# A three-part model in one kernel: zeros on TensorE ahead of the weights, block products from the third channel tile on, the router's product by halves, identity products among the last rows

## The chip, the cores and the metric

The kernel runs on one core of a Trainium2 chip. The metric is the device time of one execution in microseconds. All data is float32. Each float32 matrix product appears in the trace as two records.

## The reference, cut to what matters

For 256 tokens of 1024 values the model runs two layers and then a third block:

```
for l in range(2):
    proj = x @ w_in                        # 8 groups of columns
    q, k, v = silu(causal_dwconv(...))     # 4 taps
    o_a = gated_delta_rule(...)            # chunks of 64 tokens, 4 heads
    o_b = causal attention, 8 heads, partial rotary
    x = layer_norm(alpha * x + concat(o_a, o_b) @ w_out)
    hid = causal_dwconv(x @ w_up) + b      # 3 taps, 2 x 2816 columns
    x = layer_norm(alpha * x + (silu(gate) * val) @ w_down)
h = rms_norm(x); differential and dilated attention on h @ w_in_2
x = x + concat(oa, od) @ w_out_2
h = rms_norm(x); aff = softmax(h @ w_router)        # 16 experts
for e in range(16):                        # the 32 best tokens of each
    x[idx[e]] += ((silu(h[idx] @ w_gate[e]) * (h[idx] @ w_up[e])) @ w_down[e]) * gate
out = rms_norm(x)
```

## The kernel before, in words

All engines' instruction streams are written out by hand, in one function per engine, and joined by semaphores. SyncE (SP) streams the weights: through a ring of four slots (`slot_in0` to `slot_in3`) in the layers, and through four larger slots (`piece_in0` to `piece_in3`) for the experts. A slot is loaded again when a count of products says that it is free.

**Start.** SP loads the first column block, half of the transposed input, and the second block (semaphore `second_columns`, L401), and later, in its order, the columns of the convolution weights (L412). ScalarE's queue issues the other half of the input (L1470) and the identity constants (L1471). GpSimd's queue issues a table of distances and two small bias rows (L519 to L521), and waits for slot 1 before the other constants (L523). TensorE's `first_products` (L816) waits for the first block and goes on through L826, L813, L831, L676 to L901, L861, L909 (it needs the copied logits, L1516) and L916 (it needs ScalarE's second SiLU, L1494). ScalarE's first tap (L1482) needs the convolution columns.

**Up-products of a layer.** The 2 x 2816 hidden channels are made in 22 tiles of 2 x 128 channels. The first `AHEAD` = 3 tiles are direct: `up(j, t)` (L1098, instructions of L676) takes 16 products of 128x128 for one half t of the tokens, so 32 for the tile, into the banks `UP_BANKS`. From the fourth on a tile is made by seven block products (`up_block_products`, L1101, instructions of L1123) of four 128x128 products each, so 28. They need sums of weight blocks, which GpSimd makes tile by tile (`up_sums`, L526; four instructions, L536 to L541, with drains between), and sums of token blocks, which VectorE makes once (L2082 to L2087). VectorE joins the seven results (`up_summed`, L2094) into a bank, from where ScalarE (L1615) and VectorE (L2126) convolve. GpSimd begins once the output product is done; in layer 1 it first issues eleven DMAs (L586 to L598).

The x rows of the second half of the tokens come later from the layer norm than those of the first. So TensorE first makes `up(0, 0)` and `up(1, 0)`, then waits for `x_rows`, transposes the second half (`second_tile`, L661), makes `up(2, 0)`, and waits for the transposed copies (L666). Then follow the three second halves, and the block tiles with j = 3 on.

**Router.** The output product of the third block (L1261) makes two halves of tokens of two halves of columns each, k by k with both column halves inside. VectorE adds both column halves to x (`second_rows`, L2200), TensorE transposes x (`rows_transposed`, L1231), one copy goes to ScalarE (L1648) and one to VectorE (L2211), and TensorE makes the logits (L1244). `keep_clock` (L1248) issues products with the identity, whose results nobody reads: one behind the logits, four behind the affinities' transposes (L1270). VectorE selects the tokens (L2242, L2244), and the rows are gathered.

**Experts.** Expert 0 begins with L1348. SP loads a slot again when `piece_used` has counted its last product. The last half of the last expert's rows comes in four loads (L508, `LAST_ROWS`), with a semaphore each; TensorE's `down_rows` (L1312, instructions of L1316) takes them as they land.

Of the kernel before, what the change touches and what calls it, by code (L numbers as in the profile page):

```python
# [12 lines left out]
P = 128  # L13
S = 256
T = S // P
# [56 lines left out]
UP_BANKS = (0, 1, 4)  # L72
PAIR_BANKS = {0: (4, 5), 1: (0, 1)}
FIRST_PAIR_BANKS = (6, 7)
# [7 lines left out]
AHEAD = 3  # L82
ROWS_BANKS = (2, 3, 6, 7)
H2_BANKS = (0, 1, 4, 5)

HID_BANKS, OUT_BANK = (3, 4, 6), (4, 0)
# [82 lines left out]
def build(nc, a, out, scratch, CAT):  # L169
    ctx = ExitStack()  # L170
    with ctx:
# [125 lines left out]
        normed_rows = second_scratch.take(T, D)  # L297
        out_quarters = second_scratch.take(D // 4)
# [219 lines left out]
        def _(pool):  # L518
            pool.dma_start(bucket_table[0:BUCKETS + 1, :], a["bias_table"]).then_inc(sem("bias_in"), 16)  # L519
# [124 lines left out]
        def _(pe):  # L644
# [196 lines left out]
            for l in range(DEPTH):  # L841
# [259 lines left out]
                def up_block_products(j):  # L1101
# [57 lines left out]
            for n in range(AHEAD):  # L1159
                if n % 2 == 0:  # L1160
                    unit_in(L, n // 2)
                if n == AHEAD - 1:
# [4 lines left out]
            for n in range(AHEAD):  # L1167
# [63 lines left out]
            def rows_transposed(t):  # L1231

                pe.wait_ge(sem("second_rows"), t + 1)
                for kh in range(2):
# [4 lines left out]
            def logits(t, ks):  # L1239

                if ks[0] == 0:
                    pe.wait_ge(sem("h2_copied"), 2 * t + 2)
                for k in ks:
                    last = mm(ps[2 + t][:, 0:NE], xT[:, k, t * P:(t + 1) * P], router_w[:, k, :], start=(k == 0), stop=(k == KT - 1))  # L1244
# [9 lines left out]
            for t in range(T):  # L1254
                for k in range(4):
                    if t == 0:
                        pe.wait_ge(sem("attended_read"), at(L, "attended_read", k + 1))
                    elif k == 1:
                        rows_transposed(0)
                    for nh in range(2):  # L1260
                        last = mm(ps[ROWS_BANKS[2 * t + nh]][:, :], mixT[:, 4 + k, t * P:(t + 1) * P], slot(7, 1024)[:, k, nh * 512:(nh + 1) * 512], start=(k == 0), stop=(k == 3))  # L1261
                last.then_inc(sem("rows_used" if t else "rows_t0"), 2 if t else 1)
            logits(0, range(6))
            rows_transposed(1)
            logits(0, range(6, KT))
            logits(1, range(KT))
            keep_clock(1)
# [40 lines left out]
            def keep_clock_on_rows():  # L1308

                mm(ps[1][:, :], ident, normed_rows[:, 0, 0:512], start=True, stop=True)  # L1310
# [16 lines left out]
            def expert(n_, ahead):  # L1327
# [102 lines left out]
        def _(act):  # L1430
# [39 lines left out]
            act.dma_start(xT[:, 0:4, :], a["x_t"][:, 0:4, :]).then_inc(sem("xT_in0"), 16)  # L1470
            act.dma_start(const[:, 0:2 * P + 4], a["consts"][:, 0:2 * P + 4]).then_inc(sem("ident_in"), 16)  # L1471
            for l in range(DEPTH):
# [131 lines left out]
                for j in range(FT):  # L1604
# [4 lines left out]
                    else:  # L1609
                        act.wait_ge(sem("up_summed"), at(l, "up_summed", j - AHEAD + 1))  # L1610
                        act.wait_ge(sem("hidden_ready"), at(l, "hidden_ready", j - 2))
# [22 lines left out]
            def rms(n, t):  # L1634
# [3 lines left out]
                elif n == 1:  # L1638
                    act.wait_ge(sem("second_rows"), t + 1)
# [6 lines left out]
                if n == 1:  # L1646
                    act.wait_ge(sem("h2_transposed"), 2 * t + 1)
# [68 lines left out]
        def _(v):  # L1716
# [148 lines left out]

            for l in range(DEPTH):
# [227 lines left out]
                def up_summed(j):  # L2094

                    pair = FIRST_PAIR_BANKS if j == AHEAD else PAIR_BANKS[j % 2]
# [103 lines left out]
            def second_rows(t):  # L2200
# [3 lines left out]
                else:  # L2204
                    v.wait_ge(sem("rows_used"), (DEPTH + 1) * ROW_UNITS + 2)
                for nh in range(2):
                    xs = x[:, t, nh * 512:(nh + 1) * 512]
                    last = w.tensor_add(xs, xs, ps[ROWS_BANKS[2 * t + nh]][:, :])
                last.then_inc(sem("second_rows"), 1)
                v.wait_ge(sem("h2_transposed"), 2 * t + 2)  # L2210
                w.tensor_copy(xT[:, 4:8, t * P:(t + 1) * P], ps[H2_BANKS[2 * t + 1]][:, :].rearrange("p (x y) -> p x y", y=P)).then_inc(sem("h2_copied"), 1)  # L2211
# [137 lines left out]
```

## Time and profile before

| | |
|---|---|
| median of 3 runs | 2190.2 us (2189.45 to 2190.91) |
| profiled execution, own time | 2190.44 us |
| its span | 2188.7 us |
| TensorE busy | 1678.1 us, 77% |
| VectorE busy | 644.2 us, 29% |
| ScalarE busy | 310.7 us, 14% |
| GpSimd busy | 255.5 us, 12% |
| moved by DMA | 695.12 MB, mean 318 GB/s |

Times in the views are microseconds from the start of the span. "PE" is TensorE's products, "PEld" its weight loads, "DVE" VectorE, "ACT" ScalarE, "POOL" GpSimd, "SPq" the queue of SyncE. The granted clock is a share of 2.4 GHz, so that 0.50 is the lower level, 1.2 GHz. A row in brackets, as [0.33 <-DVE arena L1854], gives the idle time before the group and what ended it. `x32` is a count of records.

### The profile page before, as it was taken

To read this page: it belongs to the slowest core of one execution; us is meant where nothing else is said; L and a number is where in the kernel's file an instruction comes from. 1 tells how busy PE (TensorE), PEld (TensorE's weight loads), DVE (VectorE), ACT (ScalarE), POOL (GpSimd) and SP (SyncE) were. 2 spreads that over 40 slices of the span, in tenths; PEclk is the share of its full clock that TensorE was granted. 3 is DMA by queue.
4 is the path that set the end of the run, shared out by engine and by line. 5 is a ranking of instruction groups with operands and counts; after the bars stand their busy time and mean duration, and the time that the engine had idled before them with its cause. 6 is when DMAs were issued, how large, how long until landed. Compare 5 with 4: busy or idle time off the path is not lost.

```text
span 2188.7 us, 30640 instructions
## 1 busy us (share of the span) xinstructions
PE 1678.1 (77%) x13062; PEld 968.0 (44%) x13062; DVE 644.2 (29%) x1520; ACT 310.7 (14%) x739; POOL 255.5 (12%) x221
## 2 busy tenths in 40 slices
PE   8999999999999999995665565665656466466566
PEld 7867994886799476441221221221122122122122
DVE  3345777545477734320110010010010010010011
ACT  3231220324122013310000000000000000000001
POOL 0003880001388000000000000000000000000000
PEclk9999999999999999987777777777787777778778
DMA  8234652723554275489999999999999999999998
GB/s 316 79 116 145 215 181 96 255 79 116 164 173 175 96 263 235 200 374 430 433 433 434 431 427 434 435 435 434 433 426 433 435 435 434 434 431 427 435 434 345
DMA packets 99943, 695.12 MB, mean 318 GB/s; under 512 B 7627, under 2 KB 53067, under 8 KB 85773
## 3 DMA queue, kind: packets, MB, share of 16 engines
q1 hardware_dynamic: 96304, 684.71, 76.0%
q0 software_dynamic: 1712, 5.35, 0.7%
q10 hardware_dynamic: 1836, 3.80, 0.5%
q8 instruction: 64, 1.05, 0.2%
q14 instruction: 27, 0.21, 0.0%
HBM read 692.77 MB, written 4.22 MB: 318 GB/s over the span
## 4 chain that ended last, share of the span: by engine, by line
DMA 49%; PE 48%; DVE 1%; SPq 1%; ACT 1%; issue 0%; DVEq 0%; ACTq 0%
DMA arena<-in_gate_up 32%; DMA arena<-in_down_rows 17%; PE bank L1123 11%; PE bank L702 6%; PE bank L861 6%; PE bank L1348 6%; PE bank L676 3%; PE bank L1316 2%; PE bank L856 1%; PE bank L1182 1%; PE bank L1063 1%; PE bank L1186 1%; PE bank L1083 1%; PE bank L766 1%; PE bank L813 1%; PE bank L1209 1%
## 5 line engine op out<-in xcount | busy, mean ns | idle before, releaser
L1348 PE MATMUL bank<-arena 128*32 128x512 f32 (+1 forms) x3072 | 441.9, 741 | 366.0 <-DMA arena<-in_gate_up 365.5
L1348 PEld LDWEIGHTS bank<-arena 128*32 128x32 f32 x3072 | 112.5, 139 | 690.5 <-DMA arena<-in_gate_up 395.6
L2290 DVE TENSOR_TENSOR arena<-arena,bank 64x256 f32<-64x256 f32 x96 | 51.3, 535 | 766.3 <-ACT arena L1696 764.7
L1316 PE MATMUL bank<-arena 128*32 128x256 f32 x2816 | 204.5, 458 | 68.6 <-DMA arena<-in_down_rows 68.6
L1123 PE MATMUL bank<-arena 128*128 128x128 f32 x2128 | 238.0, 274 | 0.0
L1123 PEld LDWEIGHTS bank<-arena 128*128 128x128 f32 x2128 | 237.8, 192 | 0.0
L1316 PEld LDWEIGHTS bank<-arena 128*32 128x32 f32 x2816 | 101.0, 130 | 175.4 <-DMA arena<-in_down_rows 86.3
L861 PE MATMUL bank<-arena 128*128 128x256 f32 x576 | 138.6, 387 | 0.0
L1696 ACT ACTIVATE arena<-bank 64x512 f32<-64x512 f32 (+1 forms) x48 | 23.2, 550 | 809.0 <-PE bank L1348 809.0
L702 PE MATMUL bank<-arena 128*128 128x512 f32 x308 | 133.2, 592 | 0.0
L861 PEld LDWEIGHTS bank<-arena 128*128 128x128 f32 x576 | 104.7, 189 | 18.9 <-issue 4.6
L702 PEld LDWEIGHTS bank<-arena 128*128 128x128 f32 x308 | 57.8, 189 | 73.2 <-issue 70.1
L676 PE MATMUL bank<-arena 128*128 128x128 f32 (+1 forms) x704 | 87.0, 285 | 1.4 <-DVE arena L1770 1.4
L676 PEld LDWEIGHTS bank<-arena 128*128 128x128 f32 x704 | 84.1, 191 | 5.1 <-DVE arena L1770 2.6
L2126 DVE SCALAR_TENSOR_TENSOR arena<-bank,arena 128x254 f32<-128x254 f32 (+1 forms) x176 | 76.8, 478 | 24.8 <-ACT arena L1615 18.7
L1615 ACT ACTIVATE arena<-bank,arena 128x256 f32<-128x256 f32 x88 | 45.0, 562 | 139.0 <-DVE bank L2109 119.2
L536 POOL TENSOR_TENSOR arena<-arena 128x512 f32<-128x512 f32 x38 | 49.6, 1305 | 101.4 <-PE bank L1083 71.9
L1358 PE MATMUL bank<-arena 128*128 128x128 f32 x96 | 24.4, 342 | 48.3 <-DVE arena L2290 48.3
L539 POOL TENSOR_TENSOR arena<-arena 128x512 f32<-128x512 f32 x38 | 53.7, 1413 | 0.0
L2295 DVE COPY arena<-bank 64x256 f32<-64x256 f32 x16 | 6.9, 430 | 155.5 <-PE bank L1316 155.5
L538 POOL TENSOR_TENSOR arena<-arena 128x512 f32<-128x512 f32 x38 | 49.2, 1295 | 13.9 <-issue 8.6
L541 POOL TENSOR_TENSOR arena<-arena 128x512 f32<-128x512 f32 x38 | 49.6, 1306 | 5.4
(322 smaller groups left out, 1595.0 us busy)
## 6 DMA issues: line engine op xcount, KB each, us to landing
arena<-in_gate_up SPq DMA_DIRECT2D x60, 5632.0 KB, 46.2
arena<-in_down_rows SPq DMA_DIRECT2D x29, 5632.0 KB, 46.1
arena<-in_w_up SPq DMA_DIRECT2D x44, 1024.0 KB, 7.8
arena<-in_w_in SPq DMA_DIRECT2D x36, 1024.0 KB, 9.3
arena<-in_w_down SPq DMA_DIRECT2D x16, 1024.0 KB, 6.9
arena<-in_gate_up SPq DMA_DIRECT2D x5, 2816.0 KB, 12.3
arena<-in_w_out SPq DMA_DIRECT2D x12, 1024.0 KB, 6.1
arena<-in_w_down SPq DMA_DIRECT2D x12, 512.0 KB, 3.7
```

The source lines that it names most:

```text
L536: nc.gpsimd.tensor_tensor(s1, w[:, 0:4, cg], w[:, 4:8, cg], ALU.add)
L538: nc.gpsimd.tensor_tensor(s2, s1, w[:, 0:4, cv], ALU.subtract)
L539: nc.gpsimd.tensor_tensor(w[:, 0:4, cg], w[:, 0:4, cv], w[:, 0:4, cg], ALU.subtract)
L541: nc.gpsimd.tensor_tensor(s4, w[:, 4:8, cv], s2, ALU.subtract)
L676: last = mm(ps[bank][:, j * S + lo:j * S + lo + n], w[:, k, c:c + P], xT[:, k, lo:lo + n], start=(k == 0), stop=(k == KT - 1))
L702: return mm(ps[PRODUCT_BANK[m]][:, :], left, right, start=(i == 0), stop=(i == KP - 1))
L861: last = mm(ps[bank][:, j * S:(j + 1) * S], slot(u, 512)[:, k, c:c + P], xT[:, k, :], start=(k == 0), stop=(k == KT - 1))
L1123: last = mm(ps[pair[b]][:, at_ * P:(at_ + 1) * P], left[:, k, :], right[:, k, :], start=(k == 0), stop=(k == 3))
L1316: done = mm(ps[5][32 * q:32 * q + 32, 0:256], hidden_t[:, r, 32 * half:32 * half + 32], weights[:, r - shift, 256 * q:256 * q + 256], star ...
L1348: last = mm(ps[b][32 * q:32 * q + 32, 0:n], expert_x[:, k, :], weights[:, c:c + n], start=(k == 0), stop=(k == KT - 1))
L2126: last = w.scalar_tensor_tensor(ff_conv[:, j % 3, gv, s:S], from_, conv_w[:, 48 + c:49 + c], ff_conv[:, j % 3, gv, s:S], ALU.mult, ALU.add)
L2290: last = w.tensor_mul(hidden[64 * odd:64 * odd + 64, 2 * b:2 * b + m, :], blocks(expert_gate[0:64, c0:c0 + n]), blocks(ps[b][64:P, 0:n]))
```

## The change

Six edits go together:

- `START_PRODUCTS`: five products of 256 columns and one of 128 with zeros as both operands, into bank 7, before TensorE's first wait for weights. VectorE writes the zeros first of all.
- GpSimd's and ScalarE's queues wait for `second_columns` before the bias tables and the identity constants.
- `AHEAD` is 2 in the layers (the third block keeps 3 as `SECOND_AHEAD`). Tile j = 2 is made by block products: product 1 ahead of the x1 transposes, product 2 behind them, the other five after the two direct tiles' second halves. GpSimd and VectorE make one tile's sums more in each layer. Tile j = 3 now uses the banks of the first two tiles and waits for `up_convolved` 2.
- The output product of the third block goes by column halves for the second half of the tokens, and so do the adds, the transposes, the copies (both by VectorE) and the logits.
- `keep_clock` behind the logits has 256 columns in place of 512.
- Three identity products of 512 columns follow the first of the last four groups of rows.

```diff
-UP_BANKS = (0, 1, 4)
+UP_BANKS = (0, 1)
-FIRST_PAIR_BANKS = (6, 7)
-AHEAD = 3
+AHEAD = 2
+SECOND_AHEAD = 3
+START_PRODUCTS = (S, S, S, S, S, P)
...
         def _(pool):
+            pool.wait_ge(sem("second_columns"), 16)
             pool.dma_start(bucket_table[0:BUCKETS + 1, :], a["bias_table"]).then_inc(sem("bias_in"), 16)
...
+                pe.wait_ge(sem("zeros_ready"), 1)
+                for n in START_PRODUCTS:
+                    mm(ps[7][:, 0:n], zeros[:, 0:P], zeros[:, 0:n], start=True, stop=True)
                 pe.wait_ge(sem("first_columns"), 16)
...
-                    pair = FIRST_PAIR_BANKS if j == AHEAD else PAIR_BANKS[j % 2]
-                    for m in (1, 2, 4, 5, 6, 7, 3):
+                    pair = PAIR_BANKS[j % 2]
+                    for m in ms:
...
+                unit_in(l, U_UP)
                 for j in range(AHEAD):
-                    if j % 2 == 0:
-                        unit_in(l, U_UP + j // 2)
-                    if j == AHEAD - 1:
-                        second_tile(l, 1)
                     up(j, 0)
+                unit_in(l, U_UP + 1)
+                up_block_products(AHEAD, (1,))
+                second_tile(l, 1)
+                up_block_products(AHEAD, (2,))
                 second_tile_copied(l, 1)
                 for j in range(AHEAD):
                     up(j, 1).then_inc(sem("up_product"), 1)
                 pe.wait_ge(sem("x1_copied"), at(l, "x1_copied", 5))
-                for j in range(AHEAD, FT):
+                up_block_products(AHEAD, (4, 5, 6, 7, 3)).then_inc(sem("up_product"), 1)
+                for j in range(AHEAD + 1, FT):
                     if j % 2 == 0:
                         unit_in(l, U_UP + j // 2)
-                    if AHEAD < j <= AHEAD + 2:
-                        pe.wait_ge(sem("up_convolved"), at(l, "up_convolved", AHEAD if j == AHEAD + 1 else 2))
-                    elif j > AHEAD + 2:
+                    if j == AHEAD + 1:
+                        pe.wait_ge(sem("up_convolved"), at(l, "up_convolved", AHEAD))
+                    else:
                         pe.wait_ge(sem("up_summed"), at(l, "up_summed", j - 2 - AHEAD + 1))
...
-            for t in range(T):
+            def second_product(t, k, nh):
+                return mm(ps[ROWS_BANKS[2 * t + nh]][:, :], mixT[:, 4 + k, t * P:(t + 1) * P], slot(7, 1024)[:, k, nh * 512:(nh + 1) * 512], start=(k == 0), stop=(k == 3))
+            for k in range(4):
+                pe.wait_ge(sem("attended_read"), at(L, "attended_read", k + 1))
+                for nh in range(2):
+                    last = second_product(0, k, nh)
+            last.then_inc(sem("rows_t0"), 1)
+            for nh in range(2):
                 for k in range(4):
-                    if t == 0:
-                        pe.wait_ge(sem("attended_read"), at(L, "attended_read", k + 1))
-                    elif k == 1:
+                    if nh == 0 and k == 2:
                         rows_transposed(0)
-                    for nh in range(2):
...
+                    last = second_product(1, k, nh)
+                if nh == 0:
+                    last.then_inc(sem("rows_t0"), 1)
+            last.then_inc(sem("rows_used"), 2)
+            rows_transposed(1, 0)
+            logits(0, range(2))
+            rows_transposed(1, 1)
+            logits(0, range(2, KT))
             logits(1, range(KT))
-            keep_clock(1)
+            keep_clock(1, 2)
...
                             last = down_rows(half, rows_, r0, n)
+                            if i == 0:
+                                for _ in range(3):
+                                    keep_clock_on_rows(4)
...
             act.dma_start(xT[:, 0:4, :], a["x_t"][:, 0:4, :]).then_inc(sem("xT_in0"), 16)
+            act.wait_ge(sem("second_columns"), 16)
...
+            w.memset(zeros, 0.0).then_inc(sem("zeros_ready"), 1)
```

## Rows read from the trace of the kernel before

**Rows 1.** The page: engines in the chain of waits, DMA use in 40 slices:

```profile
DMA 49%; PE 48%; DVE 1%; SPq 1%; ACT 1%; issue 0%; DVEq 0%; ACTq 0%
...
DMA  8234652723554275489999999999999999999998
```

**Rows 2.** Timeline of the start: start us, us, engine, line, operation, [idle before <-releaser]:

```profile
5.79 9.74 PE L826 MATMUL bank<-arena 128*128 128x256 f32 x32 [5.79 <-DMA arena<-in_first_in]
...
15.37 7.09 PE L813 MATMUL bank<-arena 128*128 128x256 f32 x32
...
27.16 1.57 ACT L1482 ACTIVATE arena<-bank,arena 128x256 f32<-128x256 f32 x4 [10.26 <-DMA arena<-in_conv_columns]
...
32.16 0.38 ACT L1516 ACTIVATE arena<-bank 128x256 f32<-128x256 f32 x1
...
33.41 0.63 PE L909 MATMUL bank<-arena 128*64 128x4 f32 x16
...
34.26 1.15 PE L916 MATMUL bank<-arena 128*64 128x64 f32 x32 [0.22 <-ACT arena L1494]
```

**Rows 3.** Windows, TensorE: from:to, length, busy us (records begun), clock, DMA share, GB/s:

```profile
9.00:11.00 2.00, 2.00 (x6) 1.00 1.02 432
...
12.00:14.00 2.00, 2.00 (x11) 1.00 1.05 401
...
20.00:60.00 40.00, 39.78 (x342) 1.00 0.74 273
```

**Rows 4.** Timeline of the up-products' start in layer 0:

```profile
194.19 1.06 PE L657 MATMUL bank<-arena 128*128 128x128 f32 x8 [0.33 <-DVE arena L1854]
```

**Rows 5.** Chain of waits in layer 1's up-products: start us, us, what, records:

```profile
580.88 0.87 PE bank L657 x8
...
581.76 14.29 PE bank L676 x128
...
596.05 118.81 PE bank L1123 x1064
```

**Rows 6.** Timeline of the up-products' start in layer 1:

```profile
580.32 0.56 POOL L598 DMA_DIRECT2D arena<-in_norm_columns  x1
...
590.82 1.28 POOL L538 TENSOR_TENSOR arena<-arena 128x512 f32<-128x512 f32 x1 [8.63 <-issue]
...
592.52 1.02 ACT L1615 ACTIVATE arena<-bank,arena 128x256 f32<-128x256 f32 x2 [2.55 <-PE bank L676]
...
593.47 1.28 POOL L541 TENSOR_TENSOR arena<-arena 128x512 f32<-128x512 f32 x1
...
593.57 1.82 DVE L2126 SCALAR_TENSOR_TENSOR arena<-bank,arena 128x255 f32<-128x255 f32 x4 [1.75 <-ACT arena L1615]
```

**Rows 7.** Timeline of the router:

```profile
931.23 2.38 PE L1244 MATMUL bank<-arena 128*128 128x16 f32 x16 [0.43 <-DVE arena L2211]
...
933.44 2.05 PE L1251 MATMUL bank<-arena 128*128 128x512 f32 x2
...
935.29 0.63 PE L1270 MATMUL bank<-arena 128*16 128x128 f32 x2
```

**Rows 8.** Windows of the router, busy us of all engines, then clock, DMA share, GB/s:

```profile
933.00:939.00 6.00, 6.00 (x11) 2.71 (x12) 3.85 (x17) 0.57 (x4) 0.00 (x0) 0.50 0.96 400
...
942.00:943.00 1.00, 0.88 (x8) 0.48 (x8) 0.64 (x4) 0.00 (x0) 0.00 (x0) 1.00 0.00 0
```

**Rows 9.** Timeline of the last expert's last rows:

```profile
2170.20 1.93 PE L1316 MATMUL bank<-arena 128*32 128x256 f32 x32 [0.44 <-DMA arena<-in_down_rows]
...
2175.10 4.86 PE L1316 MATMUL bank<-arena 128*32 128x256 f32 x56 [2.96 <-DMA arena<-in_down_rows]
```

**Rows 10.** The line L508: issues of its four loads, time to landing:

```profile
L508 SPq DMA_DIRECT2D arena<-in_down_rows x4: 328/432/433, 2132.8 to 2134.1; - x4
...
DMA to landing us min/median/max: 37.4/42.9/44.6
```

**Rows 11.** Window of the last rows, TensorE, columns as in rows 3:

```profile
2175.20:2178.00 2.80, 2.80 (x28) 0.50 0.39 159
```

More of the change, by code:

```diff
@@ L297, in build @@
         normed_rows = second_scratch.take(T, D)
+        zeros = normed_rows[:, 0, 0:S]
         out_quarters = second_scratch.take(D // 4)
@@ L1158, in _ @@
             pe.wait_ge(sem("x0_copied"), at(L, "x0_copied", 1))
-            for n in range(AHEAD):
+            for n in range(SECOND_AHEAD):
                 if n % 2 == 0:
                     unit_in(L, n // 2)
-                if n == AHEAD - 1:
+                if n == SECOND_AHEAD - 1:
                     pe.wait_ge(sem("h1_rows"), 2)
@@ L1166, in _ @@
             pe.wait_ge(sem("x1_copied"), at(L, "x1_copied", 2))
-            for n in range(AHEAD):
+            for n in range(SECOND_AHEAD):
                 channels(n // 2, 2 * (n % 2), SECOND_BANKS[n], t=1).then_inc(sem("projected_2"), 1)
@@ L1229, in _, with rows_transposed @@
             attention(L, SECOND_PAIRS, {i: lambda i=i: second_fill(i) for i in range(20)}, {15: diff_outputs_transposed})
-            def rows_transposed(t):
-                pe.wait_ge(sem("second_rows"), t + 1)
-                for kh in range(2):
+            def rows_transposed(t, half=None):
+                for kh in range(2) if half is None else (half,):
+                    pe.wait_ge(sem("second_rows"), t + 1 + (kh if t else 0))
                     for k in range(4):
@@ L1241, in logits @@
                 if ks[0] == 0:
-                    pe.wait_ge(sem("h2_copied"), 2 * t + 2)
+                    pe.wait_ge(sem("h2_copied"), 2 * t + (1 if t else 2))
                 for k in ks:
+                    if t and k == KT // 2:
+                        pe.wait_ge(sem("h2_copied"), 4)
                     last = mm(ps[2 + t][:, 0:NE], xT[:, k, t * P:(t + 1) * P], router_w[:, k, :], start=(k == 0), stop=(k == KT - 1))
@@ L1306, in _, with keep_clock_on_rows @@
             gathered_transposed(1)
-            def keep_clock_on_rows():
-                mm(ps[1][:, :], ident, normed_rows[:, 0, 0:512], start=True, stop=True)
+            def keep_clock_on_rows(bank=1):
+                mm(ps[bank][:, :], ident, normed_rows[:, 0, 0:512], start=True, stop=True)
             def down_rows(half, weights, r0, n, shift=0):
@@ L1638, in rms @@
                 elif n == 1:
[L1639 removed]
+                    act.wait_ge(sem("second_rows"), 2 * t + 1)
                 else:
@@ L1645, in rms @@
                     f(normed_rows[:, t, :], x[:, t, :], ACT.Square, accum_out=sum_sq[:, t:t + 1])
-                if n == 1:
-                    act.wait_ge(sem("h2_transposed"), 2 * t + 1)
+                if n == 1 and t == 0:
+                    act.wait_ge(sem("h2_transposed"), 1)
                     f(xT[:, 0:4, t * P:(t + 1) * P], ps[H2_BANKS[2 * t]][:, :].rearrange("p (x y) -> p x y", y=P), ACT.Copy).then_inc(sem("h2_copied"), 1)
@@ L2094, in up_summed @@
                 def up_summed(j):
-                    pair = FIRST_PAIR_BANKS if j == AHEAD else PAIR_BANKS[j % 2]
+                    pair = PAIR_BANKS[j % 2]
                     v.wait_ge(sem("up_product"), at(l, "up_product", j + 1))
@@ L2203, in second_rows @@
                     v.wait_ge(sem("rows_t0"), at(L, "rows_t0", 1))
-                else:
-                    v.wait_ge(sem("rows_used"), (DEPTH + 1) * ROW_UNITS + 2)
                 for nh in range(2):
+                    if t:
+                        v.wait_ge(*((sem("rows_used"), (DEPTH + 1) * ROW_UNITS + 2) if nh else (sem("rows_t0"), at(L, "rows_t0", 2))))
                     xs = x[:, t, nh * 512:(nh + 1) * 512]
                     last = w.tensor_add(xs, xs, ps[ROWS_BANKS[2 * t + nh]][:, :])
-                last.then_inc(sem("second_rows"), 1)
-                v.wait_ge(sem("h2_transposed"), 2 * t + 2)
-                w.tensor_copy(xT[:, 4:8, t * P:(t + 1) * P], ps[H2_BANKS[2 * t + 1]][:, :].rearrange("p (x y) -> p x y", y=P)).then_inc(sem("h2_copied"), 1)
+                    if t or nh:
+                        last.then_inc(sem("second_rows"), 1)
+                for kh in range(2):
+                    if t or kh:
+                        v.wait_ge(sem("h2_transposed"), 2 * t + kh + 1)
+                        w.tensor_copy(xT[:, 4 * kh:4 * kh + 4, t * P:(t + 1) * P], ps[H2_BANKS[2 * t + kh]][:, :].rearrange("p (x y) -> p x y", y=P)).then_inc(sem("h2_copied"), 1)
                 if t == 1:
```

10 lines of the change are left out of this document (3 added, 7 removed).

## The prediction

> **What bounds the kernel now.** I read the page's chain of waits first. It ends with DMA 49% and PE 48% of the span [rows 1]: two halves. Up to about 945 us TensorE is busy nearly everywhere, and the loads keep up; behind it the slices of DMA use stand at 9 [rows 1], and the 16 experts run at the rate at which their weights arrive. The question for every step ahead of the experts is then whether its time is passed on. It is: the windows show no byte moving at 942 to 943 us [rows 8], since the queue waits for TensorE to free the slots of expert 0. Whatever shifts expert 0 shifts the whole stream behind it and the end. So I add changes on TensorE's path up to 945 us one to one, and I look at the last expert apart. The profiled execution took 2190.44 us (span 2188.7 and 1.7 around it), 0.2 above the median of 2190.2; the sum is made against the first and 0.2 comes off.
>
> **1. Zeros ahead of the weights, and the constants held back.** The 32 records of L826 take 9.74 us, the 32 equal ones of L813 7.09 [rows 2]. The windows name it: 6 records start in 9 to 11 us, 11 in 12 to 14 us [rows 3]. The clock column reads 1.00 in both, which it can't be in the first: by the rate it is the 1.2 GHz level, then 2.4. Zeros keep TensorE busy in the 5.79 us in which it stood idle, so L826 should run like L813: a lead of 9.74 - 7.09 = 2.65 us. Where does the lead end? ScalarE's first tap (L1482) waits 10.26 us for the convolution columns, whose load lands at 27.16; from there taps and SiLU lead to L916 at 34.26, which waits for ScalarE's L1494 [rows 2]. L909 wants the logits that L1516 copies until 32.54 [rows 2]. TensorE arrives at 33.41 - 2.65 = 30.8 instead, and stands until 32.6, does 0.63 us of tiny products, and stands again until 34.26. The columns' load stands behind the same bytes in either order: the 0.2 MB of constants and bias tables that now wait are still moved ahead of it. The lead is worth nothing: 0, with ends at -0.3 (the bytes moved late, some of which could fall behind) and, if the clock falls in the wait, plus a cold stretch (part 3). The wait on the second columns at the head of GpSimd's and ScalarE's queues holds only DMAs that are wanted after 22 us and taps that wait until 27.16 anyway.
>
> In the Trainium skill, the page "DMA: Bandwidth & Descriptors" (Queues, rings and completion order) says that each DMA engine takes packets in turn from the queues that have work. By it, the first weights would land somewhat earlier without the other two queues. That speaks against the zeros: they fill 11 records, and products that are ready would stand behind them. It is all swallowed by the same wait at L916, so by the rule too the sum is 0.
>
> **2. The third channel tile by block products, in two layers.** A record of 128x128 costs 118.81/1064 = 0.1117 us, and 14.29/128 gives the same [rows 5]. The direct tile has 64 records, the block tile 7x4x2 = 56: 8 x 0.1117 = 0.89 us less in each layer. Layer 0: the x1 transposes waited 0.33 us for the norm (L1854) [rows 4]; the 8 records put ahead of them cover it and its latency, some 0.5 us. Layer 0: -1.4 (ends -0.9 and -1.6).
> The first new wait is the one for the sums: the tile needs GpSimd's sums of j=2 at its fourth product, one tile's place earlier than j=3 did. In layer 0 no DMA stands ahead of them in GpSimd's queue, and they are in time. In layer 1 it first issues its DMAs up to L598 at 580.32. Its first sum starts at 580.9, the second instruction (L538) only at 590.82, 8.63 us idle with "issue" as the cause, and the last (L541) ends at 593.47 + 1.28 = 594.75 [rows 6]. Only the drain stands between; it behaves as if it waited for those DMAs. Before, j=3 wanted these sums at 596.05 + 24 x 0.1117 = 598.7, 4 us later. After: transposes start at 580.88 + 0.89, then 0.87 for them [rows 5], 8 records 0.89, 64 records 7.15, 8 records of product 4 0.89: TensorE is at the wait at 591.6. It stands 3.2 us. The next tile's sums come one GpSimd tile later and are just in time. Layer 1: +3.2 - 0.9 = +2.3 (ends -0.9 if the drain is short this time, +2.6). Behind the waiting product are all block products; DVE, ScalarE and GpSimd wait with them.
> The other new wait, L1123's j=3 for up_convolved 2 (its banks are those of the first two tiles): ScalarE's L1615 starts right behind the second tile's product at 592.52 and DVE's taps end at 593.57 + 1.82 [rows 6], 2.9 us behind it, while TensorE has 40 records, 4.5 us, of j=2 to do. Cost 0 (0 to +0.5). One more summed tile on DVE lies beside TensorE's work and costs nothing.
>
> **3. Clock falls.** A wait of 2.96 us ahead of L1316 at 2175.10 is followed by records at clock 0.50, the lower level, and 56 records took 4.86 us, where 32 took 1.93 at the full one, so 56 would take 3.38: such a fall costs 1.5 us [rows 9, 11]. The router's stretch of small records ends in one at 0.50 for over 6 us [rows 8], of which half is lost, 3.2 us: the other end. Two new waits can cause one: the 3.2 us in layer 1, and the start's 30.8 to 34.3 with 0.63 us of tiny records in it. For each I say a little over one in two; each costs 1.5 (0 to 3.2), and nothing hides it, as TensorE has 39.78 us of work in the 40 us from 20 to 60 us [rows 3] and no other wait in the blocks. I take one of them, +1.5, since one is the likeliest count.
> The Trainium skill's page "TensorE: Matmul & The Clock Gate" (Part 1) says that the number of cold matmuls of one kernel varies from run to run. No run here shows that yet. By it the falls would be a chance of the execution, and the median of the changed kernel would spread more than this one's 1.5 us.
>
> **4. Router.** The halves leave the number of records alone (32 and the transposes). Before, logits of tile 1 waited 0.43 us for a DVE copy (L1244) that came behind both adds and all transposes [rows 7]; now half of adds, transposes and copies lies beside products, and only the second half's chain is left, which six logits products cover: -0.8. keep_clock halved: its 2.05 us before the affinities' transposes (L1251, L1270 at 935.29) [rows 7] become 1.0; the affinities have a chain of their own beside them, so I count a third of it: -0.3. But the four later clock products run at 0.50 [rows 8] and could end behind DVE's selection, giving back up to 0.6. Taken: -1.0 (ends -0.3 and -1.6).
>
> **5. Identity products among the last rows.** Three of 512 columns are six records of four times 128 columns, 6 x 4 x 0.1117 = 2.7 us at full clock, and fit in the 2.96 us wait [rows 9]. The 56 records would take 56 x 1.93/32 = 3.4 instead of 4.86 us. But rows land late: the fourth load, issued at 2134.1, needs up to 44.6 us [rows 10], so 2178.7; its 8 records take 0.45 more, 2179.2, where before the end was 2179.96. So -0.7 (ends 0 and -1.0): next late is the last landing.
>
> **Sum:** 0 - 1.4 + 2.3 + 1.5 - 1.0 - 0.7 = +0.7: 2191.1 profiled, 2190.9 as the median. That is no change: about 0.2%, or 4.4 us, is what a measurement of this kernel tells from none.
>
> **Rivals.** (a) Cold waits, the slower side: both waits drop the clock and each stretch lasts like the router's. Place: L916 and L1123 of layer 1; price 2 x 3.2; it decides where each wait is over the 2.96 us of the last rows. Sum -0.8 + 6.4 = +5.6: 2195.8. For it: both waits are longer. Against: the fall that is nearest to them in kind, at the last rows, cost 1.5.
> (b) Sums in time: the 8.63 us was that execution's, and layer 1 gains 0.9, no fall: -1.4 - 0.9 - 1.0 - 0.7 = -4.0, 2186.2. If also the columns land earlier, -6: faster. Against: the DMAs ahead of the drain are unchanged.
> (c) The stream hides all: experts end at the same time, only the last rows count: 2189.5. Against: the empty queue [rows 8].
> (d) Waits but no falls: 0 - 1.4 + 2.3 - 1.0 - 0.7 = -0.8: 2189.4. Both fall, short: -0.8 + 3.0 = +2.2, 2192.4.
> (e) Zeros don't warm TensorE: then no lead, no fall at the start, everything else the same.
>
> **Chances.** Forecast (one fall) 0.40, (d) without falls 0.15, with both 0.16, (a) 0.08, (b) 0.12 (half of it beyond 0.2% with its addition), (c) 0.04, (e) goes with the first two, something not seen 0.05, to either side. Range 2186.5 to 2195.5; the forecast's own is 2189 to 2193. Faster 0.09, within 0.2% 0.81, slower 0.10.
>
> **What would show it.** L826 near 7.1 us; a wait of 1.8 us ahead of L909; L916 still near 34.3; L1123 in layer 1 with one idle of some 3.2 us released by GpSimd, or none (then b); the block products starting 1.4 us earlier in layer 0; a 0.50 stretch near 35 or 595 us; L1270 about 1 us earlier in its stage; the last records near 0.06 us each. If the experts' first load does not move with L1348's start, one to one is wrong.

## The result, and the profile after

The changed kernel takes 2195.56 us (median of 11 runs, 2194.58 to 2196.93) where the kernel before takes 2190.81 us in the same series (11 runs); the ratio is 1.0022, 95% interval 1.0015 to 1.003. It is slower by 4.75 us. The forecast was 2190.9, and the upper end of the range, 2195.5, lies just under the measured time. The span of the profiled execution went from 2188.7 to 2192.8 us, +4.1.

To see where a shift arises, take the first record of the same instructions in both traces at the seams between the stages, and subtract. This table is worked out from such records; its columns are differences to the kernel before, in us, and it has the experiments in it too:

```
                         start  layer 0  layer 1  third   router  experts |   span
changed kernel           +4.06    -1.35    +3.56    -0.01    -1.74    -0.29  |   +4.1
e1 no holds              +4.11    -1.34    +3.42    +0.76    -1.82    -0.37  |   +4.7
e2 no zeros              +0.33    -1.35    +3.79    +0.79    -1.84    -0.18  |   +1.5
e3 start as before       +0.27    -1.34    +2.31    -0.01    -0.96    +0.08  |   +0.3
e4 three direct tiles    +3.29    -0.01    +0.00    +0.55    -1.85    +6.39  |   +8.3
e5 sums first            +4.07    -1.35    -0.83    +0.90    -1.86    -0.37  |   +0.5
e6 columns early         -2.04    -1.34    +3.92    +0.01    -0.97    -0.45  |   -1.0
e7 before + columns      +0.35    +0.00    -0.01    +0.87    +0.00    -0.45  |   +0.8
e8 columns and sums      -2.38    -1.35    -0.84    +0.00    -1.74    -0.56  |   -7.0
e9 router, rows alone    +0.03    +0.01    +0.00    +0.78    -1.83    -0.40  |   -1.4
e10 fetch forward        +3.28    +0.01    +0.00    -0.01    +0.66   +13.12  |  +17.0
e11 e8 without holds     -1.83    -1.35    -0.83    +0.54    -1.85    -0.17  |   -5.6
```

"Start" reaches to the second half of layer 0's output product (L1083, after it L1089), "layer 0" from there to its down products, "layer 1" between the same two in layer 1, "third" from there to the output product of the third block, "router" to the first product of expert 0, "experts" to the end of the span; where a line's sum differs from its span, by 0.1 at most, the rest arose between the layers. The first line has the answer in its shape: the start and layer 1 lost, layer 0, the router and the experts' end won, and the losses are larger. The third block, which no edit touches, shifts by 0.5 to 0.9 us in seven of the lines: each of these has a stretch of 3.4 us at half clock there (begun between 889 and 898 us, in the record of granted clocks), which the others lack. So much comes and goes by itself.

The page of the changed kernel shows next to nothing of it. The shares of its chain of waits differ from those of before by a point at most [rows 1]:

```profile
DMA 49%; PE 47%; DVE 1%; SPq 1%; issue 1%; ACT 1%; POOL 0%; DVEq 0%; POOLq 0%; ACTq 0%
```

The timeline of its start (start us, us, engine, line, operation, [idle before <-releaser]) answers to [rows 2]:

```profile
1.20 5.06 PE L824 MATMUL bank<-arena 128*128 128x256 f32 x12 [1.20 <-DVE arena L1889]
6.06 7.38 PE L832 MATMUL bank<-arena 128*128 128x256 f32 x32
13.28 7.09 PE L816 MATMUL bank<-arena 128*128 128x256 f32 x32
...
28.93 1.57 ACT L1504 ACTIVATE arena<-bank,arena 128x256 f32<-128x256 f32 x4 [14.12 <-DMA arena<-in_conv_columns]
...
33.93 0.38 ACT L1538 ACTIVATE arena<-bank 128x256 f32<-128x256 f32 x1
...
34.46 1.02 PE L915 MATMUL bank<-arena 128*64 128x4 f32 x16 [3.07 <-ACT arena L1538]
...
36.03 1.97 PE L922 MATMUL bank<-arena 128*64 128x64 f32 x32 [0.55 <-ACT arena L1516]
```

The zeros work in the way that the prediction said: the first 32 records take 7.38 instead of 9.74 us, and the record of granted clocks has the full clock from 6.5 us on instead of 11.0. They begin 0.27 us later, right behind the zeros, so that the second group begins 2.09 us earlier where 2.65 had been counted. But ScalarE's first tap, which waits for the convolution columns, starts at 28.93 instead of 27.16, TensorE stands 3.07 us, and then L922, whose 32 records took 1.15 us at the full clock, takes 1.97. The windows of TensorE (from:to, length, busy us (records begun), granted clock, DMA share, GB/s) name it, there and in layer 1 and in the router, and show the full clock among the last rows:

```profile
34.00:36.00 2.00, 1.02 (x16) 0.50 1.05 386
36.00:40.00 4.00, 3.97 (x37) 0.50 1.05 388
...
594.00:596.70 2.70, 0.27 (x3) 1.00 0.75 242
597.00:600.00 3.00, 3.00 (x16) 0.50 1.08 365
600.50:604.00 3.50, 3.50 (x34) 1.00 0.11 35
932.00:938.00 6.00, 6.00 (x41) 1.00 1.02 432
938.50:941.50 3.00, 2.77 (x8) 0.50 1.08 466
2176.50:2183.00 6.50, 5.83 (x62) 1.00 0.65 267
```

From 597 to 600 us TensorE is busy without a gap and begins 16 records; from 600.5 to 604, again without a gap, 34: the half clock in numbers. In layer 0 nothing waits (compare [rows 4]):

```profile
197.75 1.06 PE L1129 MATMUL bank<-arena 128*128 128x128 f32 x8
198.65 1.04 PE L660 MATMUL bank<-arena 128*128 128x128 f32 x8
199.52 1.06 PE L1129 MATMUL bank<-arena 128*128 128x128 f32 x8
```

In layer 1 (timeline, GpSimd's part; it answers to [rows 6]) the sums of the third tile stand about as long as before behind GpSimd's own loads (7.99 us without work, 8.63 before), and TensorE, which wants them some 7 us earlier in the layer than before, waits. The last packet of these 12 loads (one more than the text on the kernel before counts) ends at 591.71 us, and the second instruction of the sums starts 1.05 us behind it; in the kernel before it is 589.76 and again 1.06 us (packets of GpSimd's queue in the two traces). So it is for its own loads that GpSimd waits:

```profile
582.91 0.55 POOL L601 DMA_DIRECT2D arena<-in_norm_columns  x1
583.48 1.29 POOL L539 TENSOR_TENSOR arena<-arena 128x512 f32<-128x512 f32 x1
592.76 1.27 POOL L541 TENSOR_TENSOR arena<-arena 128x512 f32<-128x512 f32 x1 [7.99 <-issue]
...
595.40 1.27 POOL L544 TENSOR_TENSOR arena<-arena 128x512 f32<-128x512 f32 x1
```

The costliest groups of the page say what came of that (group, busy us, mean ns | idle before, releaser): the only idle time of the block products in the whole execution is that one.

```profile
L1129 PE MATMUL bank<-arena 128*128 128x128 f32 x2240 | 253.0, 276 | 2.5 <-POOLq L545 2.5
```

The router (timeline; compare [rows 7]) has no wait within the logits of tile 1 any more, but a new one, of 0.84 us, for VectorE's selection of the tokens. The last 56 records (compare [rows 9]) run at the full clock, but in three pieces, each behind a landing:

```profile
935.41 3.31 PE L1254 MATMUL bank<-arena 128*128 128x16 f32 x28
938.56 1.20 PE L1261 MATMUL bank<-arena 128*128 128x256 f32 x2
939.61 0.38 PE L1288 MATMUL bank<-arena 128*16 128x128 f32 x1
...
945.52 0.29 PE L1295 MATMUL bank<-arena 16*128 16x16 f32 x2 [0.84 <-DVEq L2274]
...
2174.92 1.93 PE L1334 MATMUL bank<-arena 128*32 128x256 f32 x32
2176.78 2.84 PE L1328 MATMUL bank<-arena 128*128 128x512 f32 x6
2179.79 1.94 PE L1334 MATMUL bank<-arena 128*32 128x256 f32 x32 [0.16 <-DMA arena<-in_down_rows]
2182.23 1.07 PE L1334 MATMUL bank<-arena 128*32 128x256 f32 x16 [0.51 <-DMA arena<-in_down_rows]
2183.47 0.64 PE L1334 MATMUL bank<-arena 128*32 128x256 f32 x8 [0.17 <-DMA arena<-in_down_rows]
```

### The profile page after: what moved, and what is told of

It reads as the page before. It is cut to its first block, busy times and chain, and to the rows that moved or that the text cites. A ratio compares the mean times of both kernels' runs of the same rounds, so it can differ in the third digit from the quotient of the medians.

```text
span 2192.8 us, 30679 instructions
## 1 busy us (share of the span) xinstructions
PE 1676.5 (76%) x13064; PEld 969.7 (44%) x13064; DVE 647.6 (30%) x1536; ACT 310.4 (14%) x738; POOL 265.1 (12%) x229
## 4 chain that ended last, share of the span: by engine, by line
DMA 49%; PE 47%; DVE 1%; SPq 1%; issue 1%; ACT 1%; POOL 0%; DVEq 0%; POOLq 0%; ACTq 0%
DMA arena<-in_gate_up 32%; DMA arena<-in_down_rows 17%; PE bank L1129 11%; PE bank L867 6%; PE bank L705 6%; PE bank L1366 6%; PE bank L679 2%; PE bank L1334 2%; PE bank L1190 1%; PE bank L862 1%; PE bank L1069 1%; PE bank L1194 1%; PE bank L1089 1%; PE bank L769 1%; PE bank L816 1%
## 5 line engine op out<-in xcount | busy, mean ns | idle before, releaser
L1129 PE MATMUL bank<-arena 128*128 128x128 f32 x2240 | 253.0, 276 | 2.5 <-POOLq L545 2.5
L679 PE MATMUL bank<-arena 128*128 128x128 f32 (+1 forms) x576 | 72.8, 287 | 1.4 <-DVE arena L1793 1.4
L539 POOL TENSOR_TENSOR arena<-arena 128x512 f32<-128x512 f32 x40 | 52.1, 1303 | 94.0 <-PE bank L1089 71.9
L1376 PE MATMUL bank<-arena 128*128 128x128 f32 x96 | 24.0, 337 | 48.6 <-DVE arena L2317 48.6
L542 POOL TENSOR_TENSOR arena<-arena 128x512 f32<-128x512 f32 x40 | 56.4, 1411 | 0.0
L541 POOL TENSOR_TENSOR arena<-arena 128x512 f32<-128x512 f32 x40 | 51.3, 1283 | 13.5 <-issue 8.0
L544 POOL TENSOR_TENSOR arena<-arena 128x512 f32<-128x512 f32 x40 | 52.1, 1302 | 5.7
```

The lines of the kernel that those rows point to most:

```text
L539: nc.gpsimd.tensor_tensor(s1, w[:, 0:4, cg], w[:, 4:8, cg], ALU.add)
L541: nc.gpsimd.tensor_tensor(s2, s1, w[:, 0:4, cv], ALU.subtract)
L542: nc.gpsimd.tensor_tensor(w[:, 0:4, cg], w[:, 0:4, cv], w[:, 0:4, cg], ALU.subtract)
L544: nc.gpsimd.tensor_tensor(s4, w[:, 4:8, cv], s2, ALU.subtract)
L679: last = mm(ps[bank][:, j * S + lo:j * S + lo + n], w[:, k, c:c + P], xT[:, k, lo:lo + n], start=(k == 0), stop=(k == KT - 1))
```

## The experiments

**Taking the start and the third tile back.** Four kernels, each the changed kernel with one part undone. The "holds" are the waits for `second_columns` ahead of the bias tables and constants; a "stand" is a wait of TensorE in mid-stream. e1 takes out the two holds, e2 the zero products, e3 both:

```
e1:  -  pool.wait_ge(sem("second_columns"), 16)
     -  act.wait_ge(sem("second_columns"), 16)
e2:  -  pe.wait_ge(sem("zeros_ready"), 1)
     -  for n in START_PRODUCTS: mm(ps[7][:, 0:n], zeros[:, 0:P], zeros[:, 0:n], ...)
     -  w.memset(zeros, 0.0).then_inc(sem("zeros_ready"), 1)
```

> The changed kernel, but GpSimd and ScalarE issue the bias tables and the constants at once, as before (the two waits on the second columns are gone; the zeros stay). Theory H, held-back bytes: the constants moved behind the first weights push the convolution columns back, which landed at 28.93 us instead of 27.16, and this alone lengthens the stand of TensorE at the gate logits to 3.07 us, behind which the clock fell for 6.8 us. Then here the columns land near 27.2, the stand is shorter by 1.8 us, and the time falls by 1.8 (fall stays) to 4 us (fall gone too): 2191.6 to 2193.8. Rival Z, the zeros' lead itself: the columns' landing follows from the earlier reads of the weights or is chance; then they still land near 28.9 and the time stays at 2195.6.

> The changed kernel without the six zero products on TensorE; the two waits that hold back constants and bias tables stay. Theory H (held-back bytes delay the columns): the columns land near 28.9 us all the same, but the first products take 9.7 us again and so TensorE stands for about 0.5 to 1 us instead of 3.07 ahead of the gate selection; no fall of the clock there; start +1.8 against before instead of +4.06, time 2193.3. Theory Z (the zeros delay them or the landing is chance): columns near 27.2, start as before, time 2191.5.

> The changed kernel with the whole start as before: no zeros, nothing held back; layers, router and last rows stay changed. Both theories of the start expect its whole +4.06 us gone: 2195.6 - 4.1 = 2191.5. Rival, the chip passes the shift on only in part (the experts' weights set the end): less than 2 us gained, 2193.6 or more.

Measured: e1 2194.96 us (ratio to before 1.0017, 1.0008 to 1.0026), e2 2192.1 (1.0004, 0.9995 to 1.0013), e3 2191.4 (1.0001, 0.9992 to 1.001). My theory H fell: without the holds the start still loses 4.11 us, without the zeros 0.33. The first tap starts in e1 at 28.28 us, in e2 at 27.48, in e3 at 27.42 (timeline of e1, e2 and e3 in turn):

```profile
28.28 1.57 ACT L1502 ACTIVATE arena<-bank,arena 128x256 f32<-128x256 f32 x4 [12.95 <-DMA arena<-in_conv_columns]
```
```profile
27.48 1.57 ACT L1501 ACTIVATE arena<-bank,arena 128x256 f32<-128x256 f32 x4 [10.75 <-DMA arena<-in_conv_columns]
```
```profile
27.42 1.57 ACT L1499 ACTIVATE arena<-bank,arena 128x256 f32<-128x256 f32 x4 [10.11 <-DMA arena<-in_conv_columns]
```

So it is the zeros that make the columns late, by 0.9 to 1.5 us, and not the 0.2 MB held back by themselves. That was odd, since zeros move no byte. The packets of the columns' load show how: of its 128 packets, 120 end by 26.8 us in the changed kernel, and 8, one engine's share of 16, only at 28.1 to 28.3, each right behind the other; in the kernel before all 128 end by 26.5. By this pattern one DMA engine had something else to do first. (In e1, where the lateness is smallest, only 3 of the packets end behind 26.9 us, the last at 27.6.) The view of DMA queues from 22 to 24 us of the changed kernel has a row that the same view of the kernel before and of e3 does not have, a 16 KB fetch of instructions:

```profile
q8 instruction: 1, 0.02, 3.4%
```

It starts at 22.4 us; in the kernel before it starts at 28.2, in e3 at 29.1, in e2 at 27.8, and in e1 at 23.1. The 12 records of zeros stand ahead of everything, so TensorE reaches the place in its code at which the next block is fetched earlier, by its lead and by 12 records, and the fetch goes ahead of the columns.

e4 puts the third tile back to direct products in both layers (`AHEAD` = 3 with its banks and waits):

> The changed kernel with the third channel tile by direct products again, in both layers (three direct tiles, their banks and waits as before); start, router and last rows stay changed. By the shifts between the two traces the part costs +3.55 us in layer 1 (GpSimd's sums late and a clock fall) and gives 1.36 us in layer 0: 2195.6 - 2.2 = 2193.4. Rival: the fall in layer 1 was chance of that execution, the part costs 0.7 only: 2194.9. In its trace no record of a half clock near 597 us and no wait on GpSimd's sums.

Measured: 2197.09 us, slower than the changed kernel, so by the time alone both expectations failed. By the trace the first held: layer 1 shifts by 0.00 and has no stretch at half clock, and expert 0 begins 2.5 us earlier than in the changed kernel. Then the experts take 6.39 us longer. The cause stands in the view of DMA queues over the experts (945 to 2190 us): e4, and below it the changed kernel:

```profile
q8 instruction: 41, 0.67, 0.2%
```
```profile
q8 instruction: 13, 0.21, 0.1%
```

The loop over pairs of experts runs without fetching TensorE's code again in the changed kernel; in e4 three of its passes fetch it, and TensorE stands (waits: engine, line, us in total, times, longest):

```profile
PE bank L1365 <- issue: 15.2, 2, 8.0
```

The starts of the experts' products show where the time goes: against the kernel before, e4 is 2.2 us late at 1152 us, 5.1 at 1472, still 5.1 at 1739 and 9.1 at 2112. The lateness grows in the three passes that fetch, by 2.3 us a pass; in the kernels that don't fetch it stays within 0.2 us over the same stretch. How a fetch costs that much is only partly shown. The 28 fetches more are 0.46 MB and take 2 us of the 16 engines' time. The rest isn't a pause of the stream, as it would be if TensorE freed its slots too late: from 1150 to 2110 us the packets fill the 16 engines' time in e4 as they do in the changed kernel (packet times of all queues, divided by 16: 962.3 us in both, fetches included). What is left, argued and not shown, is that a load is complete only when its last engine is, and that fetches keep single engines behind. Nor is it the same in every execution, it seems: the eleven runs of e4 spread over 7.7 us, those of the changed kernel over 2.4.

**The two repairs.** Two edits, each on the stage that lost, and one of them on the kernel before as a control:

```
columns early (e6, e7, e8), ahead of first_blocks(2, 4), which loads the rest of the first weights:
     +  if l == 0:
     +      sp.dma_start(conv_w, a["conv_columns"][l]).then_inc(sem("conv_in"), 16)
        (and at its old place:  if l: sp.dma_start(conv_w, ...))
sums first (e5, e8), GpSimd in layer 1:
        pool.wait_ge(sem("rows_used"), DEPTH * ROW_UNITS + 1)
     +  feed_forward_sums(DEPTH - 1)
        pool.dma_start(first_gain, ...) and its 11 further loads
     -  feed_forward_sums(DEPTH - 1)
```

> The changed kernel; in layer 1 GpSimd forms all sums of the feed forward ahead of its 12 small loads instead of behind them (layer 0 and all else as in the changed kernel). Theory D, GpSimd's drain behind its own loads makes the sums late: TensorE's wait of 2.50 us ahead of the fourth product of the third tile and the 3.4 us at half clock behind it go, layer 1 comes out 0.9 us shorter than before instead of 3.55 longer: -4.4, 2195.6 - 4.4 = 2191.2. Rival, the sums are late by themselves (GpSimd starts them as late and each takes as long; or the weights of the third tile land late): the wait stays within 1 us of its size, 2195.

> The changed kernel; in layer 0 the load of the convolution columns (112 KB) is issued right behind the second block of the first weights, ahead of all further weights. What runs e1 to e3 suggest: with zeros the columns land at 28.3 to 28.9 us, without them at 27.2 to 27.5, whether or not the constants are held back; and in the runs with zeros a 16 KB fetch of TensorE's instructions stands at 22.4 to 23.0 us, just ahead of the columns' packets, in those without at 27.8 to 29.0. If the columns' landing is what swallows the lead, the taps start near 14 us, the gate logits are copied near 30, no stand ahead of the gate selection, no fall near 34, and the block at L929 starts at 40.4 instead of 46.3: 2195.6 - 5.9 = 2189.7. Rival, the constants on GpSimd's queue (landing near 28.2) or the decay chain on the other engines are just behind the columns: a third of it, 2193.5.

> The kernel before, with the load of the convolution columns issued right behind the second block of the first weights. If in the kernel before TensorE itself is the path (it waited 0.22 us ahead of L916), this alone gives 0.2 us and the lead of the zeros is what the early columns make useful: 2190.6. Rival, the columns were the path already: the start 1 us or more shorter, 2189.7; or the 112 KB ahead of the weights delay the first products by 0.3: 2191.0.

> The changed kernel with both repairs: the columns' load early and in layer 1 the sums ahead of GpSimd's loads. If both stand by themselves the gains add: 2195.6 - 4.4 - 5.9 = 2185.3, 5.5 us under the kernel before. Rival, the experts' stream does not pass the second half on: 2187.5 or more.

Measured: e5 2190.92 us (0.9998, 0.9989 to 1.0007), e6 2189.64 (0.999, 0.9981 to 0.9999), e7 2190.98 (0.9997, 0.9988 to 1.0006), e8 2183.99 (0.9967, 0.9955 to 0.9979). The first theory of e5 and of e6 holds within 0.3 us, and their rivals fell. In e5 the fourth block product of the third tile starts at 593.23 us and the others follow with no wait and no half clock; layer 1 is 0.83 us shorter than before, where 0.89 had been counted. In e6 TensorE goes through the start without a stand, though the fetch is still at 22.6 us (timeline):

```profile
28.67 1.08 PE L910 MATMUL bank<-arena 128*32 128x256 f32 x16
29.67 2.00 PE L870 MATMUL bank<-arena 128*128 128x256 f32 x8
31.60 0.64 PE L918 MATMUL bank<-arena 128*64 128x4 f32 x16
32.09 1.13 PE L925 MATMUL bank<-arena 128*64 128x64 f32 x32
33.15 7.20 PE L870 MATMUL bank<-arena 128*128 128x256 f32 x32
```

Without zeros the early columns are worth nothing (e7: start +0.35): the kernel before had TensorE itself as its path there [rows 2]. In e7 it was a rival that came true, not the first theory: the 112 KB ahead of the weights delay the first products, by 0.5 us (5.79 in [rows 2]; timeline of e7), and the wait of 0.22 us ahead of L916 is all that they give:

```profile
6.29 9.98 PE L829 MATMUL bank<-arena 128*128 128x256 f32 x32 [6.29 <-DMA arena<-in_first_in]
```

Lead and early columns pay only together, -1.8 to -2.4 (e6, e8, e11). In e8 the gains add, and 1.3 us more comes than was expected, of which 0.8 is the router's shorter stretch at half clock (3.4 us, where e6 has 6.8). It beats the kernel before, in its own series, by 6.9 us and the changed one by 11.6.

**The controls.** e9 is the kernel before with the router part and the identity products alone. e10 is the kernel before with 16 products of 16 columns of zeros behind the first two blocks. e11 is e8 without the holds.

```
e10: +  for _ in range(16):
     +      mm(ps[7][:, 0:16], zeros[:, 0:P], zeros[:, 0:16], start=True, stop=True)
```

> The kernel before with the router part and the identity products among the last rows alone; start and both layers as before. The shifts of the other traces give 1.74 us for the router and 0 to 0.3 at the end: 2190.8 - 1.9 = 2188.9. It is also the control of e4, which likewise had three direct tiles and fetched TensorE's instructions 28 times more within the loop of the experts (two stands of 8.0 us): if three direct tiles by themselves bring that, it shows here too, 2193 or more; if it hangs on where the loop comes to lie behind the code ahead of it, it doesn't.

> The kernel before, with 16 narrow products of zeros (16 columns, 32 records) right behind the first two blocks: no lead, nothing held back, but 32 records more ahead of the place at which TensorE's next 16 KB of instructions are fetched, which moves from 28.2 us to about 22. Theory F, the fetch stands ahead of the columns' packets on one of the 16 DMA engines: 8 of the 128 packets come 1 to 1.5 us behind the others and the first tap moves from 27.2 to 28.3 us or later, as in the runs with zeros. Rival, the zeros' lead or the earlier reads of weights slow the load: the tap stays at 27.2 to 27.5. Time: 1.8 us of narrow products more on TensorE's path, 2192.6.

> The kernel of e8 (changed kernel, columns' load early, sums ahead of GpSimd's loads) without the two waits that hold back bias tables and constants. With zeros in both, the first products took 7.38 us with the waits (changed kernel) and 7.91 without (e1): if nothing swallows it now, 2184.0 + 0.5 = 2184.5. Rival: the held-back constants land last now and the waits cost as much, 2184.0.

Measured: e9 2188.89 us (0.9991, 0.9981 to 1.0; the gain is at the edge of what can be told), as expected, with 13 fetches over the experts. So it isn't the three direct tiles that made e4 fetch its loop again. e4 and e9 have the same code on TensorE in the loop and differ ahead of it, in 12 records of zeros and their wait (and, on other engines, in the holds).

e10: theory F holds. There is no lead and nothing is held back; the fetch starts at 23.8 us, 120 of the columns' packets end by 26.4 as before and 8 at 27.7 to 28.0, and the first tap moves from 27.16 to 28.74 (timeline):

```profile
28.74 1.57 ACT L1486 ACTIVATE arena<-bank,arena 128x256 f32<-128x256 f32 x4 [11.90 <-DMA arena<-in_conv_columns]
```

Its time I missed by 13 us: 2205.85 (2 runs). The narrow products took 3.64 us instead of 1.8, and the start shifts by 3.28; 13.12 us more arise within the experts. Of these, 2.5 come before 1150 us, behind a stretch of 6.8 us at half clock that begins at 946 us; then every pass of the loop fetches its code (DMA queues over the experts):

```profile
q8 instruction: 66, 1.08, 0.4%
```

From 1150 to 2110 us, where the other kernels fetch nothing (e8 one block), e4 fetches 27 blocks in three passes, e10 54 in all six. By the starts of the experts' products e10 is 6.4 us late at 1152 us and 15.7 at 2112, 1.6 us a pass, where e4 lost 2.3 in each of its three. That code added ahead of the loop brings the fetches is shown by the pairs e4 and e9, e10 and the kernel before. The records of all kernels ahead of expert 0 agree with it: 6404 to 6420 in those that don't fetch, 6432 in e4, 6452 in e10. At which amount it sets in, and why in only three passes of e4, is open.

e11: 2184.77 us (0.9971, 0.996 to 0.9983), expected 2184.5. By the medians the holds are worth 0.8 us in the repaired kernel, and 0.6 the other way in the changed one (e1 against it), where the lead is swallowed; both are near what can be told apart, but the shift of the start, -2.38 against -1.83, says the same as the first.

## Why the prediction was wrong

**The start** failed, and with it the forecast. The step was "the columns' load stands behind the same bytes in either order" and, from it, "the lead is worth nothing: 0". Measured: +4.06 us. 1.77 is the tap at 28.93 instead of 27.16: one engine had a fetch of TensorE's code ahead of its 8 packets, and e10, which moves the fetch without lead or holds, moves the tap by 1.58. L922 starts 1.77 us late by it. Another 2.1 is the half clock behind the stand: from L922's start to the block at L929 it is 10.26 us instead of 8.12. That the wait swallows the lead was right; the premise that zeros on TensorE don't touch a load was not: code is bytes too, and running ahead in the code brings its fetch forward. The statement that TensorE would stand ahead of L909 and L916 was right in kind; its 1.8 us became 3.07.

**Layer 0** was right: -1.35 for -1.4, and -1.34 or -1.35 in the seven experiments that keep the edit.

**Layer 1**: the wait was right. e3, which kept its clock, shifts by +2.31, the +2.3 of the sum; and e5, without the loads in front, has no wait at all. In the changed kernel the products behind the wait start at 596.77 us, 2.7 later than back to back, where 3.2 had been counted. With e5's -0.83 that makes +1.8 of the +3.56; the rest, 1.7, is the fall. The same working gives 1.7 for e1 and e2 and 1.5 for e6, so a fall here costs 1.5 to 1.7 us, for 1.5. (The +3.4 to +3.9 of these four are not compared with e3's +2.31 as they stand, since their waits are not equally long.)

**The falls**: the step was "I take one of them, +1.5, since one is the likeliest count". Both came, and the first was long (6.8 us at half clock, by the record of granted clocks) and cost 2.1. Of the 3.4 us by which the span's shift of 4.1 exceeds the +0.7 of the sum, the two falls, 3.9 for 1.5, are the larger part, and the late columns with 1.8 the next; layer 1 and the router gave some 0.5 and 0.7 back. Rival (a), both waits cold and each stretch as long as the router's, gave 2195.8 where 2195.56 came, but not by its own terms: its price of 3.2 each was too high, the columns' 1.8 us were missing in it, and the router gave more. It was the nearest, for half a reason. The Trainium skill's page "TensorE: Matmul & The Clock Gate" (Part 1) says that the number of cold matmuls of a kernel varies from run to run; the runs here agree as far as they can: TensorE stood 2.74 us in e2 and the clock fell, and 2.88 us at the same place in e3 and it did not (timeline of e2 and of e3 up to 605 us; 90 and 104 records begin in about the same time):

```profile
593.28 11.94 PE L1126 MATMUL bank<-arena 128*128 128x128 f32 x90 [2.74 <-POOLq L545]
```
```profile
593.37 11.88 PE L1125 MATMUL bank<-arena 128*128 128x128 f32 x104 [2.88 <-POOLq L544]
```

The spread of the runs decides nothing: 2.4 us for the changed kernel, 6.2 for the one before in the same series.

**The router**: -1.74 for -1.0. The kernels with this part fall into two groups: e3 and e6, with 6.8 us at half clock in the router like the kernel before, gain 0.96 and 0.97; those with 3.4 us there gain 1.74 to 1.86. The work moved is worth 1.0, as the sum had it, and the shorter cold stretch up to 0.8, a term that the sum lacked. It gives no more, since the four later identity products then end ahead of VectorE's selection, for which TensorE waits 0.84 us (L1295); in e3 they end last and nothing waits. The term is read from this grouping; no run sets the length of the stretch alone, and e10, with the router as before and 3.4 us there, loses 0.66 by a second fall that begins at 946.2 us, just ahead of expert 0.

**The last rows**: -0.29 for -0.7. The 56 records did run at the full clock, as said, in 4.32 us with three waits for landings, 0.84 us together, in and ahead of them. Inside the experts' stage the shift first grows from 4.4 to 4.9 us, so the end itself gives 0.8 back. But e7, which lacks the edit, gains the same 0.8 there. Its wait in these rows is 1.93 us, not 2.96, and the clock doesn't fall: the 32 records behind it take 1.93 us. So the identity products gave nothing over a kernel whose clock stayed up by itself; how often it does is open.

**One to one** held: +4.44 at expert 0 is +4.1 at the end; in e8, -6.39 is -7.0.

## What to carry to other kernels

Idle engines aren't the only thing that filler work touches: each instruction added ahead of a place brings the fetches of code behind it forward, and code added ahead of a loop can make the loop fetch itself again. So look at the row of the instruction queue, over the start and over the loop, before a time is credited to the edit. A lead is worth what the next load ahead of it allows, so pair it with an earlier issue of that load: neither of the two alone paid here, together they gave 1.8 to 2.4 us. And where an engine both issues loads and forms operands, put the operands that another engine waits for ahead of the loads.

## What the runs showed of the hardware that I had not expected

- A 16 KB fetch of TensorE's instructions took 1.09 us at 22 to 24 us in the runs with zeros (0.9 to 1.5 us elsewhere in the start). With it in front, the last 8 of the 128 packets of a 112 KB load were through 1.4 to 1.6 us behind the other 120 (changed kernel, e4, e10), and the first tap started 0.9 to 1.8 us later.
- The loop of the experts ran without fetching code again in 11 of the 13 kernels, but fetched it in three passes of e4 (12 records of zeros more ahead of it than in e9) and in all six from 1150 us on in e10 (32 more than in the kernel before), at 2.3 and 1.6 us a pass.
- GpSimd's second instruction behind a first one starts 8.0 to 8.6 us late when 12 of its loads stand ahead of both, 1.05 us behind the last packet of these loads; with the sums ahead of the loads (e5) it follows 1.4 us behind the first.
- Narrow products (16 columns, e10) took 3.64 us for 32 records, 0.114 each, about as much as the 0.112 of products of 128 columns at the full clock. The clock was full here too: the records just ahead of them, of 256 columns, started 0.21 to 0.22 us apart, and 0.43 apart in the first 4 us.
